# The RWKV recurrence of a two-block kernel: 64x64 products on all four quarters of the TensorE array

## The reference, cut to what matters

```python
def _rwkv7_recurrence(r, w, k, v, kk, b):          # 8 heads, state S is 64 x 64 per head
    def step(S, inp):
        r_t, w_t, k_t, v_t, kk_t, b_t = inp
        sa = jnp.einsum('bhvk,bhk->bhv', S, kk_t)
        S = (S * w_t[:, :, None, :] - sa[..., :, None] * b_t[:, :, None, :]
             + v_t[..., :, None] * k_t[:, :, None, :])
        return S, jnp.einsum('bhvk,bhk->bhv', S, r_t)
    _, ys = lax.scan(step, S0, xs)                  # 256 steps, S0 = 0
```

## Time and profile before

| | |
|---|---|
| median of three runs | 2547.01 us |
| the profiled execution's own time | 2550.34 us |
| its span, from the first to the last instruction | 2548.6 us |
| TensorE matmul busy | 2438.7 us, 96% of the span |
| TensorE weight loads busy | 2298.2 us, 90% |
| VectorE busy | 1667.2 us, 65% |
| ScalarE busy | 1178.2 us, 46% |
| GpSimd busy | 11.8 us |

### The profile page before, as it was taken

How to read it: one execution, slowest core, us unless ns; L and a number is a source line. 1 busy time by engine, 2 the same in 40 slices (tenths; PEclk the granted TensorE clock), 3 DMA queues, 4 the chain that set the end, 5 groups by cost and what they waited for, 6 DMA issues and landing times.

```text
span 2548.6 us, 50076 instructions
## 1 busy us (share of the span) xinstructions
PE 2438.7 (96%) x20408; PEld 2298.2 (90%) x20408; DVE 1667.2 (65%) x2657; ACT 1178.2 (46%) x1702; POOL 11.8 (0%) x28
## 2 busy tenths in 40 slices
PE   4999999999999999999999999999999999999998
PEld 4998889989998888998999999899999999998998
DVE  6777877787878556666557574665565565736555
ACT  4345354453444455445346462453454365516433
POOL 0000000000000000000000000000000000000000
PEclk9999999999999999999999999999999999999999
DMA  7775767756787314554554340345555543304543
GB/s 310 277 291 219 283 236 273 295 210 253 285 307 275 108 51 150 203 225 159 181 183 180 116 150 20 136 179 181 182 175 187 181 151 125 139 20 157 182 181 132
DMA packets 66520, 480.96 MB, mean 189 GB/s; under 512 B 7504, under 2 KB 7552, under 8 KB 9136
## 3 DMA queue, kind: packets, MB, share of 16 engines
q1 hardware_dynamic: 64656, 468.33, 50.0%
q0 software_dynamic: 1696, 10.18, 1.1%
HBM read 477.41 MB, written 1.07 MB: 188 GB/s over the span
## 4 chain that ended last, share of the span: by engine, by line
PE 53%; issue 35%; DVE 5%; ACT 5%; DMA 2%; POOL 0%; DVEq 0%; SPq 0%; ACTq 0%; POOLq 0%
PE bank L544 53%; ACT w_hi L1265 2%; DVE w_lo L1818 1%; DMA ring<-weights 1%; ACT work L1265 1%; DVE y L1852 1%; ACT sq L1265 1%; PE bank L575 1%; ACT L1265 1%; DMA rows<-row 0%; DVE work L2272 0%; ACT h_hi L1265 0%; DVE sq L2599 0%; DVE work L2597 0%; DMA sq<-rows 0%
## 5 line engine op out<-in xcount | busy, mean ns | idle before, releaser
L1818 DVE TENSOR_TENSOR w_lo<-ring,w_hi 128x1024 fp32r<-128x1024 f32 x715 | 870.4, 1223 | 592.2 <-ACT w_hi L1265 586.9
L544 PE MATMUL bank<-h_hi,w_hi 128*128 128x256 f32 x3896 | 1117.6, 287 | 36.7 <-DVE w_lo L1818 23.7
L1265 ACT ACTIVATE w_hi<-ring 128x1024 fp32r<-128x1024 f32 x726 | 763.9, 1057 | 794.3 <-PE bank L544 704.0
L544 PE MATMUL bank<-h_lo,w_hi 128*128 128x256 f32 x3896 | 1107.0, 284 | 0.0
L544 PE MATMUL bank<-h_hi,w_lo 128*128 128x256 f32 x3896 | 1106.8, 284 | 0.0
L544 PEld LDWEIGHTS bank<-h_hi,w_hi 128*128 128x128 f32 x3896 | 751.7, 193 | 51.7 <-issue 25.8
L544 PEld LDWEIGHTS bank<-h_lo,w_hi 128*128 128x128 f32 x3896 | 751.7, 193 | 3.4
L544 PEld LDWEIGHTS bank<-h_hi,w_lo 128*128 128x128 f32 x3896 | 751.4, 193 | 0.0
L544 PE MATMUL bank<-w_hi,act_hi 128*128 128x512 f32 x704 | 275.0, 391 | 0.0
L544 PE MATMUL bank<-w_lo,act_hi 128*128 128x512 f32 x704 | 274.9, 391 | 0.0
L544 PE MATMUL bank<-w_hi,act_lo 128*128 128x512 f32 x704 | 273.9, 389 | 0.0
(11 more groups left out here) (212 smaller groups left out, 1784.5 us busy)
## 6 DMA issues: line engine op xcount, KB each, us to landing
ring<-weights SPq DMA_DIRECT2D x443, 1024.0 KB, 4.8
work<-cmp POOLq DMA_DIRECT2D x1, 4096.0 KB, 14.2
sq<-rows POOLq DMA_DIRECT2D x6, 512.0 KB, 5.7
work<-lora POOLq DMA_DIRECT2D x2, 1024.0 KB, 5.1
x<-x_in SPq DMA_DIRECT2D x1, 1024.0 KB, 11.6
out<-y SPq DMA_DIRECT2D x2, 512.0 KB, 2.6
const_sb<-consts SPq DMA_DIRECT2D x1, 854.0 KB, 13.4
v_first<-c_in SPq DMA_DIRECT2D x1, 512.0 KB, 3.7
```

What stands on the lines that cost most here:

```text
L544: return nc.tensor.matmul(out, lhsT, rhs, start=start, stop=stop, skip_group_check=skip)
L1265: return nc.scalar.activation(out, in_, f, bias=bias, scale=scale, **kw)
L1818: tt(w_lo[q % SLOTS][:, :], ring[n % RING][:, c * HALF:(c + 1) * HALF], w_hi[q % SLOTS][:, :].bitcast(F32), ALU.subtract).then_inc(halves_ ...
```

## The change

It names a pair j as (h, e), j = 2h + e. For pairs with e = 0 nothing moves. For pairs with e = 1 a matmul may send its output to the other half of the partitions (`other`), and reads operands that an earlier one left there. A set is ordered (chunk, h, e, r), so four matmuls in a row are e = 0 with r = 0 and 1, and e = 1 with r = 0 and 1. Outputs of pairs with e = 0 go to one PSUM bank, of e = 1 to the next; a set takes 256 columns in each of two banks, where it took one bank of 512. By the arguments of each call:

- on four quarters: both `pairs`, `turned_tokens` 0 to 2, U at levels 2 to 5, D at levels 2 to 4, all Tr, AV, `y_v`, W, and in the state loop SA, the term of the new state, dS, and y;
- on two quarters, as before: `turned_tokens` 3, X0t, U and D at level 1, D at level 5, XK, the rho term.

The number of matmuls, of VectorE and of ScalarE operations and their sizes stay as they are. One copy of y moves from VectorE to ScalarE (into stage `gates`); both now run after the last chunk. The order of the sets that no level waits for changes: `turned_tokens` 3 of T = 0 comes between X0t_0 and X0t_1; of T = 1, token sets 0 to 3 stand at the end of level 1, inside and at the end of level 2, and at the end of level 3; KK for T = 1 moves from the end of level 2 into level 3; AV moves to level 4, `y_v(0)` to the end of level 4 and `y_v(1)` into level 5. Both W come before both XK. Further waits on TensorE: for `tok` copies before the sets that write the same banks, for Xt before U (it was before D), for `rho` before y, for y0 before rho of chunk 2, for XK_1 before the state term of chunk 0.

VectorE and ScalarE read and write the same sizes through views over two banks (`two`) or the new order of blocks (`by_chunk`); the masks of AB and KK take one parity e at a time where they took one chunk, and those of KK for T = 1 come after X at level 3.

In the diff of the TensorE program only the added lines and those around them are shown; the lines that they replace are in the code printed above.

```diff
...
+pe += [f"AB{r}_{T}" for T in halves for r in halves] + [f"turned{i}_0" for i in range(3)]
+pe += ["X0t_0", "turned3_0", "X0t_1"]
+act += [f"tok{i}_0" for i in range(3)] + ["X0_0", "tok3_0", "X0_1"]
...
+extra_pe = {1: (["KK0_0", "KK1_0"], ["turned0_1"]), 2: (["turned1_1"], ["turned2_1"]),
+        3: (["KK0_1", "KK1_1"], ["turned3_1"]), 4: (["AV_0"], ["AV_1"])}
+extra_act = {1: ([], ["tok0_1"]), 2: (["tok1_1"], ["tok2_1"]), 3: ([], ["tok3_1"]), 4: (["AV_0"], ["AV_1"])}
...
+banks = ctx.enter_context(nc.psum_tensor("bank", [P, 8 * 512], F32))
+bank = [banks[:, i * 512:(i + 1) * 512] for i in range(8)]
...
+    return t.rearrange("p (T e i h t) -> p T e i h t", T=2, e=2, i=2, h=2)
...
+def two(b, c, n=TOK):
+    return banks[:, b * 512:(b + 2) * 512].rearrange("p (e c) -> p e c", e=2)[:, :, c:c + n]
...
+def y_bank(e):
+    return bank[6 + e].rearrange("p (T h t) -> p T h t", T=2, h=2)
...
+        def blocks():
+            return [(ci, h, e, r) for ci in range(2) for h in range(2) for e in range(2) for r in range(2)]
+        def own(r, e):
+            return rows_of[r]
+        def other(r, e):
+            return rows_of[r ^ e]
         def pairs(name, b, left, T):
+            for ci, h, e, r in blocks():
+                j, c = 2 * h + e, 2 * T + ci
+                ins = mm(bank[b + e][other(r, e), (2 * ci + h) * P:(2 * ci + h + 1) * P],
+                         left[rows_of[r], j, tk(c)], kap_rho[rows_of[r], :, j, tk(c)], True, True)
+                if (ci, h, r) == (1, 1, 1):
+                    ins.then_inc(*R.pe.step(f"{name}{e}_{T}"))
+        def at(b, at_col, ci, h, e, rows_):
+            return bank[b + e][rows_, at_col + (2 * ci + h) * CH:at_col + (2 * ci + h + 1) * CH]
+        def turned_tokens(i, T, b, at_col):
             src = (khat, bhat, zp[:, 8:12, :], kap)[i]
+            to = own if i == 3 else other
+            for ci, h, e, r in blocks():
+                ins = mm(at(b, at_col, ci, h, e, to(r, e)), src[rows_of[r], 2 * h + e, tk(2 * T + ci)],
+                         K("ident")[rows_of[r], rows_of[r]], True, True)
             ins.then_inc(*R.pe.step(f"turned{i}_{T}"))
+        def product(name, b, at_col, left, right, T, source, to):
+            for ci, h, e, r in blocks():
+                i = source(r, e)
+                ins = mm(at(b, at_col, ci, h, e, to(r, e)), left[i, T, e, ci, h, 0:CH],
+                         right[i, T, e, ci, h, 0:CH], True, True)
             ins.then_inc(*R.pe.step(f"{name}_{T}"))
+        def turned_blocks(name, b, at_col, src, T, to):
+            for ci, h, e, r in blocks():
+                i = other(r, e)
+                ins = mm(at(b, at_col, ci, h, e, to(r, e)), src[i, T, e, ci, h, :], K("ident")[i, i], True, True)
             ins.then_inc(*R.pe.step(f"{name}_{T}"))
+        def y_at(T, ci, h, e, r):
+            n = T * TOK + h * P + ci * CH
+            return bank[6 + e][rows_of[r], n:n + CH]
         def y_v(T):
+            for ci, h, e, r in blocks():
+                i = other(r, e)
+                mm(y_at(T, ci, h, e, r), tok[2][i, T, e, ci, h, :], KK[i, T, e, ci, h, CH:2 * CH],
+                   T == 0 and ci == 0 and h == 0, False, True)
...
             if i == 0:
+                pe.wait_ge(*R.act.at("XK_0"))
...
         pe.wait_ge(front_taken, st.front + 24)
+        turned_tokens(0, 0, 4, 0)
+        turned_tokens(1, 0, 6, 0)
+        pe.wait_ge(*R.act.at("tok0_0"))
+        turned_tokens(2, 0, 4, TOK)
+        pe.wait_ge(*R.vec.at("X_t0_0"))
+        turned_blocks("X0t", 0, 0, X_t, 0, other)
+        pe.wait_ge(*R.act.at("tok1_0"))
+        turned_tokens(3, 0, 6, TOK)
+        pe.wait_ge(*R.vec.at("X_t0_1"))
+        turned_blocks("X0t", 2, 0, X_t, 1, other)
         for lv in range(1, LEVELS):
             for T in range(2):
                 pe.wait_ge(*(R.act.at(f"X0_{T}") if lv == 1 else R.vec.at(f"X{lv - 1}_{T}")))
+                if lv > 1:
+                    pe.wait_ge(*R.act.at(f"Xt{lv - 1}_{T}"))
+                product(f"U{lv}", 2 * T, 0, AB, X, T, other, other if lv == 1 else own)
             if lv == 1:
+                pe.wait_ge(*R.act.at("tok2_0"))
                 pairs("KK", 4, khat, 0)
             if lv == 2:
+                pe.wait_ge(*R.act.at("tok0_1"))
+                turned_tokens(1, 1, 6, TOK)
             if lv == 3:
+                pe.wait_ge(*R.act.at("tok1_1"))
+                pairs("KK", 6, khat, 1)
             if lv == 4:
+                pe.wait_ge(*R.act.at("tok3_1"))
+                product("AV", 4, 0, KK, tok[2], 0, other, own)
+            if lv == 5:
+                y_v(1)
             for T in range(2):
                 pe.wait_ge(*R.vec.at(f"U{lv}_{T}"))
+                if lv == 1:
+                    product("D1", 2 * T, TOK, X_t, U, T, other, other)
+                elif lv < LEVELS - 1:
+                    product(f"D{lv}", 2 * T, TOK, X_t, U, T, own, other)
                 else:
+                    product(f"D{lv}", 2 * T, TOK, U, X_t, T, own, own)
             if lv < LEVELS - 1:
                 for T in range(2):
                     pe.wait_ge(*R.vec.at(f"X{lv}_{T}"))
+                    turned_blocks(f"Tr{lv}", 2 * T, 0, X, T, own)
             if lv == 1:
                 pe.wait_ge(*R.act.at("tok3_0"))
+                turned_tokens(0, 1, 6, 0)
             if lv == 2:
+                pe.wait_ge(*R.vec.at("KK1_0"))
+                turned_tokens(2, 1, 4, 0)
             if lv == 3:
+                pe.wait_ge(*R.act.at("tok2_1"))
+                turned_tokens(3, 1, 4, TOK)
+            if lv == 4:
+                pe.wait_ge(*R.act.at("AV_0"))
                 pe.wait_ge(*R.vec.at("KK1_1"))
+                product("AV", 4, TOK, KK, tok[2], 1, other, own)
+                y_v(0)
         for T in range(2):
             pe.wait_ge(*R.vec.at(f"X_t{LEVELS - 1}_{T}"))
             pe.wait_ge(*R.act.at(f"AV_{T}"))
+            product("W", 2 * T, 0, X_t, av, T, own, other)
+        product("XK", 4, 0, tok[3], X_t, 0, own, own)
+        pe.wait_ge(*R.act.at("W_0"))
+        product("XK", 0, TOK, tok[3], X_t, 1, own, own)
+        pair_of = [(h, e, r) for h in range(2) for e in range(2) for r in range(2)]
         for c in range(4):
             T, cl = c // 2, c % 2
             pe.wait_ge(*(R.vec.at(f"S{c}") if c else R.pool.at("S0")))
             if cl == 0:
                 pe.wait_ge(*R.act.at(f"XK_{T}"))
+            for h, e, r in pair_of:
+                ins = mm(at(2, 0, 0, h, e, other(r, e)), xkt[rows_of[r], T, e, cl, h, :], S[rows_of[r], e, h, :],
+                         True, True)
             ins.then_inc(*R.pe.step(f"SA{c}"))
+            if c == 2:
+                pe.wait_ge(*R.pe.at("y0"))
+            for h, e, r in pair_of:
+                ins = mm(y_at(T, cl, h, e, r), S[rows_of[r], e, h, :], rho[rows_of[r], 2 * h + e, tk(c)],
+                         False, False, True)
+            ins.then_inc(*R.pe.step(f"rho{c}"))
+            if c == 0:
+                pe.wait_ge(*R.act.at("XK_1"))
+            for h, e, r in pair_of:
+                i = other(r, e)
+                mm(at(0, 0, 0, h, e, rows_of[r]), tok[0][i, T, e, cl, h, :], tok[2][i, T, e, cl, h, :],
+                   h == 0, False, True)
             fill()
             pe.wait_ge(*R.vec.at(f"san{c}"))
+            for h, e, r in pair_of:
+                i = other(r, e)
+                ins = mm(at(0, 0, 0, h, e, rows_of[r]), tok[1][i, T, e, cl, h, :], sa_neg[i, T, e, cl, h, :],
+                         False, h == 1, True)
             ins.then_inc(*R.pe.step(f"dS{c}"))
             if cl == 0:
                 fill()
                 continue
+            pe.wait_ge(*R.pe.at(f"rho{c}"))
+            for ci, h, e, r in blocks():
+                i = other(r, e)
+                ins = mm(y_at(T, ci, h, e, r), sa_neg[i, T, e, ci, h, :], AB[i, T, e, ci, h, CH:2 * CH],
+                         False, T == 1 and ci == 1 and h == 1, True)
             ins.then_inc(*R.pe.step(f"y{T}"))
...
```

More of the change, by code:

```diff
@@ L341, in build @@
         work = sb("work", 23296)
-        bank = [ctx.enter_context(nc.psum_tensor(f"bank{i}", [P, 512], F32)) for i in range(8)]
+        banks = ctx.enter_context(nc.psum_tensor("bank", [P, 8 * 512], F32))
+        bank = [banks[:, i * 512:(i + 1) * 512] for i in range(8)]
         FRONT, SPARE = (4, 5), 6
@@ L1073, in tk @@
                     return slice(c * CH, (c + 1) * CH)
-                def blocks(T):
-                    return [(ci, j, r) for ci in range(2) for j in range(4) for r in range(2)]
-                def at(b, ci, j, r):
-                    return bank[b][rows_of[r], (4 * ci + j) * CH:(4 * ci + j + 1) * CH]
-                def pairs(name, b, left, T):
-                    for ci, j, r in blocks(T):
-                        c = 2 * T + ci
-                        ins = mm(bank[b + ci][rows_of[r], j * P:(j + 1) * P], left[rows_of[r], j, tk(c)],
-                                 kap_rho[rows_of[r], :, j, tk(c)], True, True)
```

(42 more changed lines are left out.)

157 lines of the change are left out of this document (52 added, 105 removed).

## The result

The changed kernel took 2534.37 us, median of 6 runs (2530.55 to 2537.91), beside 2547.80 us for the kernel before in the same session. The ratio is 0.9943, its 95% interval 0.9933 to 0.9953: 13.4 us faster, where 34 were forecast. The execution whose profile is read here took 2531.25 us.

What follows compares the result with a forecast made beforehand. TensorE's pace on small matmuls was taken to bound both recurrences. Gains of 1.55 + 12.4 + 3.1 = 17.1 us a layer, 34 for both, take the profiled 2550.34 to 2516.3, median 2513; 8-in-10 range 2504 to 2548.

Steps and rivals of the forecast that it cites:

- What bounds the kernel: Both recurrences: bound by TensorE's pace on small matmuls, with nothing hidden behind it; 135.7 us at stake.
- The pace of four quarters: Sets of 16 matmuls on four quarters: 0.47 us instead of 0.93, records 14.6 ns apart.
- Start: Recurrence up to U1_0, 9.15 us before: DVE limits it, so the gain is 1.55 us a layer.
- State loop: Last window of the recurrence, 17.44 us before: falls to 14.3, a gain of 3.1 us a layer.
- Copies over two banks at no cost: DVE and ACT views over two banks: same element counts, taken as 0; at the far end 2.3 us a layer.
- Levels and W/XK: Middle window, U1_0 to SA0, 41.25 us before: falls to 28.9, a gain of 12.4 us a layer.
- (a): Rival: weights or the record start rate hold 29 ns a record, so only pairs gain; 2540; chance 0.20.
- the 2532 that it worked out from 25 ns between starts: Variant within (a): the skill's floor of about 25 ns between starts makes a matmul cost 50 ns; about 2532.
- (b): Rival: a row half's moving data serves one quarter at a time, so no gain; 2547; chance 0.15.
- (c): Rival: quarters sharing output columns shut each other out, 46 us a layer more; 2640; chance 0.06.
- (d): Rival: PE's idle gaps cost the clock; at 1.2 GHz in both recurrences 19 us a layer more; 2585; chance 0.05.
- PE is idle much longer than 1 us a level: Sign of error in the recurrence's levels; level 2 was forecast at 4.8 us with about 3.8 us of PE.

Runs made afterwards that it cites:

- e9: Changed kernel plus 512 one-column fp32 matmuls without waits ahead of the third norm's transposes; 2559.31 us, run once; the added stream took 28.2 us.
- e1: Changed kernel with two matmuls of a couple of heads merged into one of 128 moving columns in products and turns (other values computed); 2511.4 us, ratio 0.9857.
- e6: e5 with two matmuls of a couple of heads merged into one of 128 moving columns, as in e1; 2542.1 us, ratio 0.9986.
- e5: Changed kernel with odd pairs' output back on the quarter of their own rows, so only two quarters are used; 2546.3 us, ratio 0.9995.
- e2: Kernel before the change, on two quarters, with the same merging of matmuls as in e1; 2540.8 us, ratio 0.9973.
- e3: Changed kernel with four added one-column matmuls ahead of 44 sets a layer, 704 more instructions a layer; 2553.6 us, ratio 1.0023.
- e8: Changed kernel with X's turns made by whole-array transposes and XK and turned_tokens 3 on four quarters, 448 fewer instructions a layer; 2524.6 us, ratio 0.9905.

## Why the prediction was wrong, step by step

- **What bounds the kernel**: right in part. PE had no gap that the profile shows, but "bound by the pace at which TensorE takes its small matmuls, and nothing is hidden that a faster pace wouldn't bring out" was the error. A second limit of nearly the same size was hidden: 29.1 ns x 128 records is 3.72 us, and e9 measures 3.73 for a block. An engine that is busy all the time can stand close to two limits at once.
- **The pace of four quarters**: right, 15 ns a record. e1 against e6 shows the quarters worth 16.3 us a layer.
- **Start** (1.55 us): right, 7.5 us up to U1_0, set by DVE as worked out.
- **State loop** (14.3 us): right, 14.6 and 14.4 in e1.
- **Copies over two banks at no cost**: right, ACT and DVE took 597 and 688 ns as in the earlier trace rows, and e5 equals the kernel before.
- **Levels and W/XK** (28.9 us from U1_0 to SA0): **the step that failed**, 38.5 us measured. Its sum held for the array and the other engines: e1, where the instructions come in time, runs the same chain of sets and waits, with merged matmuls, in 27.4. What it lacked is a term for bringing the instructions. It asked 1,360 records to go in 28.9 us, 21 ns each, where blocks give 29 on average. 10.6 blocks x 3.7 = 39.3 us, about the 38.65 and 38.30 measured; instructions that were there in advance can account for the rest, which no run separates.
- **The rivals**: (a) said "the rate at which records start" holds 29 ns a record. Its figure over a long stretch was right, its mechanism (weights, or a floor under each start) wrong: records start 15 ns apart on average until a block is used up. Its price, 2540, was nearer than the forecast, and the 2532 that it worked out from 25 ns between starts was nearer still, by luck: 12 to 15 ns between starts were measured (e9, and the sets above). That 2534 lies inside the range of 2504 to 2548 is luck as well: the range reached that far for (a) and (b), and neither happened. (b) and (c) fell, as an AV set goes at 15 ns a record (neither 29 nor 58) and e5 shows that the quarters gain; (d) fell, as the clock was 1.00 in all six windows. The rule of the Trainium skill that the prediction weighed ("TensorE: Matmul & The Clock Gate", Part 3), that a weight load overlaps matmuls in flight only when the row group differs, fell with (b): with four quarters at 15 ns a record, two of one row half take weights and matmuls side by side.
- The prediction named "PE is idle much longer than 1 us a level" as what would prove it wrong, and that is what happened: 8.1 us without a releaser in the first recurrence, in eight waits.

The Trainium skill, "Runtime: NRT & Kernel Launch", section Instruction fetch mechanics, describes blocks of 16 KiB (256 instructions) through the sequencer's own DMA queue and says that crossing into the next one is mostly hidden. The size agrees with the packets here; the second half doesn't hold for the small matmuls here: e9 stood 2 us at each block. The profile before had a row that could have made me ask, in its DMA view: ten packets of the instruction queue, one per 4.0 us, in a window where nothing else moved. It shows the rate in use, not that there is none much higher; that took the runs.

## What to carry to other kernels

Before forecasting that an engine will go faster, count its instructions: on TensorE every fp32 matmul of this kernel is four (two weight loads, two matmuls), and over more than some 500 instructions TensorE was fed 256 of them per 3.7 us or so, 14.5 ns each, whatever the array could do. Small matmuls on several quarters at once pay in full only if the instructions become fewer as well: here they brought 13 us alone and 31 where matmuls were merged. Merge matmuls to more moving columns, or turn whole arrays, first. In a trace, read long waits that end on "issue" every 128 records or so, with evenly spaced packets of the instruction queue, as this limit.

## What the runs showed of the hardware

- Instructions of TensorE: a block of 256 per 3.46 to 3.73 us where nothing else moved (e9, granted clock 0.56), and 3.5 to 4.1 us in the changed kernel's recurrence at 1.00, with about two blocks in advance after a quieter stretch (253 records before the first stall).
- Other DMA traffic may delay a block. The longest stall of e9, 3.36 us before 356.57, is the one during which the weights' queue moved 1.05 MB; in the DMA view of 346 to 376 us (slices of 0.75 us) six of the seven instruction packets stand alone, and the one that is missing, of that block, is among the weights:

```profile
GB/s 0 0 0 0 22 0 0 131 229 459 404 197 0 0 0 22 0 0 0 0 22 0 0 0 0 22 0 0 0 0 22 0 0 0 0 22 0 0 0 0
...
q1 hardware_dynamic: 144, 1.05, 9.6%
q8 instruction: 7, 0.11, 1.7%
```

  It is one case; no run repeated it.
- Four 64x64 quarters really work at once, two of one row half included, weight loads too: 15.0 to 15.6 ns a record of 64 columns in the rows above, and quarters that share output columns don't shut each other out. A stream of one-column matmuls in two quarters of one row half took 1.6 us for 128 records, 12.4 ns each (e9).
- Not settled: the 2.2 us a layer that merging brings on two quarters (e2, e6), the share of the clock in e3, why the first recurrence gained less than the second in e8, and whether records of other quarters start ahead of their order. Whether the 3.7 us can be shortened, by fewer or earlier packets, wasn't tried.
